# Fixing experts 0, 4 and 8 as the first three, and loading the third's gate and up into the out product's buffers

## The chip, the cores and the metric

The kernel is one program on one core of one Trainium2 chip. What counts is the device time of one execution in microseconds, the median over runs.

## What is computed

One step of a diffusion backbone with one layer: 128 context tokens and 256 latent tokens of width 1024 go through a normalisation, two token mixers side by side, one output projection, and a mixture of experts. Everything is float32. The change touches only the last part:

```python
def _moe(h, router_w, router_b, w_gate, w_up, w_down):      # h: 384 tokens x 1024
    scores = sigmoid(h @ router_w)                          # 16 experts
    sel = scores + router_b
    g = argmax over 4 groups of the sum of the group's two best sel
    expert = the two best of the four experts of group g    # 768 (token, expert) pairs
    w = scores of the two, divided by their sum
    hg = einsum('td,edf->tef', h, w_gate)                   # w_gate, w_up: 16 x 1024 x 512
    hu = einsum('td,edf->tef', h, w_up)
    act = silu(hg) * hu * gates
    return einsum('tef,efd->td', act, w_down)               # w_down: 16 x 512 x 1024
```

Gate and up of one expert are 2.10 MB each and its down matrix is 2.10 MB too, 6.29 MB in all; the sixteen are 100.7 MB.

## The kernel before

The kernel is written by hand, engine by engine; the order on each engine is that of the code, and engines meet at semaphores. SyncE (SP) issues nearly all loads, ScalarE (ACT) issues the writes of expert outputs, GpSimd (POOL) the indirect transfers. One large SBUF array, the arena, holds everything: nine slots of 16 KB per partition (`slot(0)` to `slot(8)`) and a region F behind them. What may be loaded when depends on who used the same bytes before.

**Up to the router.** The mixers' output is multiplied by w_out (L664), six products of a token tile and a half of the columns; each adds 1 to `wo_ready`. w_out lies in slots 7 and 8. VectorE then makes the normalised tokens h2 (slot 6, three tiles of 128 tokens), the router's product and the choice of two experts per token follow, and VectorE works out for each pair its row in a list of pairs sorted by expert (L1616 to L1646).

**The order of the experts.** The sorted list doesn't follow the experts' numbers. Each expert gets a key, its pair count times 32 plus a priority (`prio`). Two fixed experts, 0 and 1, have priorities so large that they come first. The number of larger keys is the expert's rank; from the rank a turn key is made, and the number of smaller turn keys is the expert's *place*, 0 to 15, in which it is worked on. Before, the turn key is 0.15 times the rank, plus 1 for ranks 2 and 4: places 0 to 15 hold the ranks 0, 1, 3, 5, 6, 7, 8, 2, 9, 10, 4, 11, 12, 13, 14, 15. `exp_i`, `n_i` and `off_i` hold, by place, the expert's number, its count and its first row.

**The sorted tokens.** GpSimd scatters h2's rows to their sorted rows in HBM (L1906, semaphore `tok_sent`). SP reads the 768 rows back as six tiles of 128 (`hsr`, L419, `hs_in0` to `hs_in5`), here into slot 7 and half of slot 8. TensorE transposes them (`sorted_columns`, L738, `hs_ready` counts two per tile), and ScalarE and VectorE copy half each out of PSUM (L1114, L1651). The expert in place 0 doesn't wait for this: its first 128 rows are gathered by a product with a one-hot matrix (L825, `first_ready`).

**The expert loop.** A place is worked on in passes of 64 rows, up to `PASSES` = 6, as many as the count needs; the others are `skipped`, which adds what they would have added to the semaphores. A pass on TensorE is `gate_up` (32 matmuls, L754), `down` of the pass before (16 matmuls, L767) and two transposes (L777). So the down of a place's last pass runs after the first gate_up of the next place. ScalarE does silu (L1110) and evacuates the output (L1125, L1129, two writes of 128 KB), VectorE multiplies (L1661), turns over (L1666) and stages the next 64 rows (`stage_x`, L1656).

**The weights.** There are `SETS` = 3 buffers, each with two slots for gate and up and one for down; place p uses buffer p mod 3. `reload` loads place p's gate and up once place p-3 has all its gate_ups counted (`gated`), and its down once place p-3's last down is counted (`downed`). The first two experts are known beforehand and load long before the router has run. The third is whatever the keys put in place 2: SP waits until it is known, loads its gate half after the sorted tiles are read, its up half and down when they are transposed (its buffer overlaps the tiles), and goes on with `reload` for places 3 to 15.

## Time and profile before

| | |
|---|---|
| median of 3 runs | 545.04 us (544.37 to 546.21) |
| span of the profiled execution, its own time | 544.1 us |
| TensorE (PE) matmuls busy | 480.4 us, 88% |
| VectorE (DVE) busy | 236.0 us, 43% |
| ScalarE (ACT) busy | 148.2 us, 27% |
| GpSimd (POOL) busy | 104.4 us, 19% |
| mean granted TensorE clock | 0.968 |
| HBM read and written | 152.77 MB and 11.34 MB |
| SP's loads of w_gate / w_up | 32 each of 1024 KB |
| SP's loads of w_down | 16 of 2048 KB |

The span runs from the first to the last instruction of one execution; the runs' times are measured from outside. Busy time is the sum of an engine's instructions and counts no waits. In rows of the timeline, the two numbers ahead of the engine are start and length in microseconds; in brackets stands how long the engine had been idle before and what released it. PEq, SPq and ACTq are the engines' instruction queues, at branches and at the issue of transfers. The granted clock is a share of TensorE's full 2.4 GHz: 1.00 is that, 0.50 is 1.2 GHz.

### The profile page before, as it was taken

The page shows a single profiled execution, that of the slowest core. Times are in us where ns is not written, and L with a number is a line of the kernel's source. Part 1 is how long each engine was busy: PE and PEld are TensorE (multiplying, and loading weights), DVE is VectorE, ACT ScalarE, POOL GpSimd, SP SyncE. Part 2 cuts the span into 40 slices and gives each one's busy share as a digit, 9 for nine tenths or more (in the row PEclk, how much of TensorE's full clock was granted, in tenths as well). Part 3 has the DMA queues.
Part 4 walks back from the last instruction along what each step waited for, and adds up shares of the span by engine and source line. Part 5 has one row for each costly group of instructions (what it writes and reads, how often), then busy time and mean ns, then how long its engine had stood idle before and what let it go on. Part 6 is the DMA issues. An engine that isn't in the chain of part 4 may idle for free. (4 is left out here: it accounts for less than half of the span.)

```text
span 544.1 us, 8978 instructions
## 1 busy us (share of the span) xinstructions
PE 480.4 (88%) x3278; PEld 233.3 (43%) x3279; DVE 236.0 (43%) x590; ACT 148.2 (27%) x289; POOL 104.4 (19%) x187
## 2 busy tenths in 40 slices
PE   2788979899969999995996999899998999999893
PEld 1135669655559644573344333333333333333331
DVE  2698994999963300867663101111011101111045
ACT  3645794532147610151102010110001100101142
POOL 3000250988870203500500000000000000000300
PEclk9988999999999999995998999999999999999998
DMA  8993046449497999220696999999999999999932
GB/s 278 339 400 112 1 154 217 166 166 363 143 391 269 369 366 417 82 86 1 239 385 243 410 423 418 418 418 416 421 421 419 419 417 419 417 420 421 403 120 116
DMA packets 42571, 164.64 MB, mean 303 GB/s; under 512 B 3314, under 2 KB 4106, under 8 KB 32676
## 3 DMA queue, kind: packets, MB, share of 16 engines
q1 hardware_dynamic: 35440, 144.22, 67.3%
q10 hardware_dynamic: 4580, 11.91, 5.8%
q0 software_dynamic: 2512, 7.99, 4.0%
q8 instruction: 24, 0.39, 0.3%
q14 instruction: 15, 0.12, 0.1%
HBM read 152.77 MB, written 11.34 MB: 302 GB/s over the span
## 5 line engine op out<-in xcount | busy, mean ns | idle before, releaser
L754 PE MATMUL psum<-arena 128*64 128x512 f32 x672 | 150.7, 601 | 16.7 <-DVE arena L1656 7.8
L754 PEld LDWEIGHTS psum<-arena 128*64 128x64 f32 x672 | 49.8, 138 | 103.7 <-issue 101.9
L767 PE MATMUL psum<-arena 128*64 128x512 f32 x336 | 75.9, 592 | 0.0
L1661 DVE TENSOR_TENSOR arena<-arena,psum 128x256 f32<-128x256 f32 x21 | 8.8, 421 | 143.4 <-ACT arena L1110 143.2
L1916 POOL DMA_INDIRECT arena<-sorted_outputs,src_u x6 | 5.7, 951 | 244.1 <-DMA sorted_outputs<-arena 242.6
L767 PEld LDWEIGHTS psum<-arena 128*64 128x64 f32 x336 | 25.7, 137 | 45.9 <-issue 45.9
L1110 ACT ACTIVATE arena<-psum 128x256 f32<-128x256 f32 x21 | 8.0, 383 | 130.0 <-PE psum L754 114.5
L664 PE MATMUL psum<-arena 128*128 128x512 f32 x96 | 42.2, 594 | 0.0
L1125 ACT ACTIVATE arena<-psum 128x512 f32<-128x512 f32 x19 | 11.3, 597 | 58.0 <-PE psum L767 58.0
L664 PEld LDWEIGHTS psum<-arena 128*128 128x128 f32 x96 | 17.9, 190 | 21.2 <-issue 20.9
L1656 DVE COPY arena<-arena 128x512 f32 x31 | 13.1, 423 | 30.4 <-issue 30.4
L487 PE MATMUL psum<-arena 128*2 128x512 f32 x64 | 18.4, 734 | 8.1 <-DMA arena<-in_w_mod 8.1
L528 PE MATMUL psum<-arena 128*128 128x388 f32 x64 | 23.8, 521 | 1.1 <-ACT arena L957 1.1
L940 ACT ACTIVATE arena<-arena 128x512 f32<-128x512 f32 x32 | 20.9, 715 | 7.7 <-DVE arena L1371 7.7
L536 PE MATMUL psum<-arena 128*128 128x388 f32 x64 | 21.1, 491 | 0.0
L617 PE MATMUL psum<-arena 128*128 128x512 f32 x48 | 20.9, 594 | 0.0
L1666 DVE COPY arena<-psum 128x256 f32<-128x256 f32 x21 | 8.9, 425 | 25.3 <-PEq L786 13.7
L1860 POOL TENSOR_TENSOR arena<-arena 128x64 f32<-128x64 f32 x32 | 14.8, 464 | 22.3 <-DVEq L1462 19.9
L472 PE MATMUL psum<-arena 128*2 128x128 f32 x512 | 15.4, 273 | 1.4 <-DMA arena<-in_w_mod 1.4
L528 PEld LDWEIGHTS psum<-arena 128*128 128x128 f32 x64 | 12.4, 203 | 9.0 <-issue 3.0
L1862 POOL TENSOR_TENSOR arena<-arena 128x64 f32<-128x64 f32 x32 | 15.2, 476 | 2.5
L536 PEld LDWEIGHTS psum<-arena 128*128 128x128 f32 x64 | 12.1, 190 | 8.4
(355 smaller groups left out, 657.3 us busy)
## 6 DMA issues: line engine op xcount, KB each, us to landing
arena<-in_w_gate SPq DMA_DIRECT2D x32, 1024.0 KB, 15.7
arena<-in_w_up SPq DMA_DIRECT2D x32, 1024.0 KB, 18.1
arena<-in_w_down SPq DMA_DIRECT2D x16, 2048.0 KB, 15.2
arena<-in_w_mod SPq DMA_DIRECT2D x12, 2048.0 KB, 13.0
arena<-in_w_in SPq DMA_DIRECT2D x3, 2048.0 KB, 19.2
sorted_outputs<-arena ACTq DMA_DIRECT2D x38, 128.0 KB, 6.3
arena<-in_w_out SPq DMA_DIRECT2D x2, 2048.0 KB, 16.7
arena<-modulation_rows ACTq DMA_DIRECT2D x4, 1024.0 KB, 10.7
```

What stands on the lines that cost most here:

```text
L472: last = mm(out[t], sil[:, k, :], w[:, k, t * P:t * P + P], start=(k == 0), stop=False)
L487: last = mm(bank[(4, 7)[c]][32 * t:32 * t + 2, :], sil[:, k, :], w[:, kk, t * D + c * 512:t * D + c * 512 + 512], start=(k == 0), stop=(k ...
L528: last = mm(bank[c][:, 0:TOK], w[:, k, c * P:(c + 1) * P], h1T[:, k, :], start=(k == 0), stop=(k == KD - 1))
L536: last = mm(out, w[:, k, c * P:(c + 1) * P], h1T[:, k, :], start=(k == 0), stop=(k == KD - 1))
L617: last = mm(bank[b][:, :], h1T[:, k, T0[t]:T0[t] + P], w[:, k, :], start=(k == 0), stop=(k == KD - 1))
L664: last = mm(bank[OUT_BANK[2 * t + h]][:, :], yT[:, k, T0[t]:T0[t] + P], wout[h][:, k, :], start=(k == 4), stop=(k == 3))
L754: last = mm(bank[0][HALF * t:HALF * t + HALF, :], xs[:, side, k, :], gu[:, :, k, t * 256:t * 256 + 256], start=(k == 0), stop=(k == KD - 1))
L767: last = mm(bank[4][HALF * h:HALF * h + HALF, :], hiddenT[:, s * P + t * HALF:s * P + t * HALF + HALF], dn[:, 2 * t + s, h * 512:h * 512 + ...
L940: last = A(out[:, :, 16 * g:16 * g + 16], made[i % 4], ACT.Copy, scale=side[:, c:c + 1])
L1656: cp(xs[:, side], hTs[:, :, bass.ds(row, HALF)]).then_inc(S("x_staged"), 1)
L1860: p(G.tensor_tensor(pt1, prev, Tre, ALU.mult))
L1862: w(G.tensor_tensor(nxt, nxt, pt1, ALU.add))
```

## The change

- The fixed experts are 0, 4 and 8 (`EARLY`), with priorities 65536, 32768 and 16384.
- The turn key becomes rank + 1.75 for ranks 0 to 9 and half the rank from 10 on.
- The third buffer's gate and up move from slots 6 and 7 to slots 7 and 8, its down from slot 8 to slot 6. SP loads the third expert's gate and up when the sixth out product is done.
- The six sorted tiles move: tiles 0, 1 and 2 lie where h2 was, tile 3 behind it over the router's small arrays, tile 4 in region F, and tile 5 shares tile 0's place. SP loads tiles 0, 1, 2, 4, then 3; ScalarE issues the load of tile 5 after tile 0 is transposed.
- Place 3's gate and up are issued when place 0 is counted off, ahead of the wait for the transposed tiles; the third's down comes after that wait, place 3's down when its buffer is free.
- On TensorE the branches of place 0 are rearranged: with two passes it counts the missing passes off between the second gate_up and its down, and again ahead of the sorted tiles' transposes, which now stand inside the branch.

```diff
--- before.py
+++ after.py
@@ -52,6 +52,7 @@
 OUT_BANK = (4, 5, 6, 7, 0, 1)
 SORT_BANK = ((1, 5), (6, 7), (3, 5), (6, 7), (3, 5), (6, 7))
 UNIT = 4096
+EARLY = (0, 4, 8)
 EPS = 1e-6
 PI = 3.141592653589793
 BIG = 1.0e30
@@ -162,7 +163,7 @@
         g2rows = view(slot(0) + 6144, 2, D)
         h2 = view(slot(6), NT, D)
         h2T = view(F + 3072, KD, NT * P)
-        hsr = view(slot(7), 6, D)
+        hsr = [view(at, D) for at in (slot(6), slot(6) + 1024, slot(6) + 2048, slot(6) + 3072, F + 12544, slot(6))]
         hTs = view(F + 3072, KD, READ)
         xs = view(F + 10752, 2, KD, HALF)
         first_rows = [view(F + 12544 + 512 * i, 512) for i in range(2)]
@@ -179,8 +180,8 @@
 
 
         def expert_weights(j):
-            b = (3, 0, 6)[j]
-            return view(slot(b), 2, KD, DE), view(slot(b + 2), 4, D)
+            gu, dn = ((3, 5), (0, 2), (7, 6))[j]
+            return view(slot(gu), 2, KD, DE), view(slot(dn), 4, D)
 
         cur = [F + 14928]
 
@@ -407,30 +408,36 @@
 
             sp.wait_ge(S("y_ready"), 4)
             sp.wait_ge(S("fin_done"), 1)
-            load_gate_up(0, 0)
-            load_down(0, 0)
+            load_gate_up(0, EARLY[0])
+            load_down(0, EARLY[0])
             sp.wait_ge(S("unit_used"), 15)
-            load_gate_up(1, 1)
+            load_gate_up(1, EARLY[1])
             sp.wait_ge(S("yt_done"), 4)
             sp.wait_ge(S("modd_in5"), 32)
-            load_down(1, 1)
+            load_down(1, EARLY[1])
+            sp.wait_ge(S("wo_ready"), 6)
+            load_gate_up(2, EARLY[2])
+
+            def load_sorted(t):
+                sp.dma_start(hsr[t], hsd[t * P:(t + 1) * P, :]).then_inc(S(f"hs_in{t}"), 16)
+
             sp.wait_ge(S("tok_sent"), 16 * 6)
-            for t in range(6):
-                sp.dma_start(hsr[:, t, :], hsd[t * P:(t + 1) * P, :]).then_inc(S(f"hs_in{t}"), 16)
-            sp.wait_ge(S("first_ready"), 1)
+            sp.wait_ge(S("pad_sent"), 48)
+            sp.wait_ge(S("first_ready"), 4)
+            for t in (0, 1, 2):
+                load_sorted(t)
+            load_sorted(4)
             sp.wait_ge(S("onehots_done"), 1)
-            sp.wait_ge(S("pad_sent"), 48)
             sp.wait_ge(S("int_done"), 1)
-            third = expert_at(2)
-            for k, sem in ((0, "gu_in2"), (KD // 2, "gu_rest2")):
-                sp.dma_start(expert_weights(2)[0][:, 0:1, k:k + KD // 2],
-                             wg[:, bass.ds(third, 1), k:k + KD // 2, :]).then_inc(S(sem), 16)
+            load_sorted(3)
+            fourth = expert_at(SETS)
+            sp.wait_ge(S("gated"), PASSES)
+            load_gate_up(0, fourth)
             sp.wait_ge(S("hs_ready"), 12)
-            for k, sem in ((0, "gu_in2"), (KD // 2, "gu_rest2")):
-                sp.dma_start(expert_weights(2)[0][:, 1:2, k:k + KD // 2],
-                             wu[:, bass.ds(third, 1), k:k + KD // 2, :]).then_inc(S(sem), 16)
-            load_down(2, third)
-            for e in range(SETS, NE):
+            load_down(2, EARLY[2])
+            sp.wait_ge(S("downed"), PASSES + 1)
+            load_down(0, fourth)
+            for e in range(SETS + 1, NE):
                 reload(e % SETS, e)
             sp.wait_ge(S("columns_copied"), 1)
             for ri, name in enumerate(("out_re", "out_im")):
@@ -736,7 +743,7 @@
                     for kk in range(4):
                         k = 4 * h + kk
                         last = tr(bank[SORT_BANK[t][h]][:, kk * P:(kk + 1) * P],
-                                  hsr[:, t, :].rearrange("p (q k) -> p k q", k=KD)[:, k, :], ident[:, :])
+                                  hsr[t].rearrange("p (q k) -> p k q", k=KD)[:, k, :], ident[:, :])
                     last.then_inc(S("hs_ready"), 1)
 
             pe.wait_ge(S("exp_done"), 1)
@@ -839,16 +846,43 @@
             pe.wait_ge(S("first_staged"), 2)
             pe.wait_ge(S("x_staged"), 2)
             first_n = pe.value_load(n_i[0:1, 0:1], min_val=0, max_val=NT * P)
+
+            def sorted_tiles():
+
+                for t in range(6):
+                    sorted_columns(t)
+                pe.wait_ge(S("hs_copied_a"), 6)
+                pe.wait_ge(S("hs_copied_v"), 6)
+
             with pe.If(first_n > HALF):
-                second_pass(0, 0, 0)
-            for t in range(6):
-                sorted_columns(t)
-            pe.wait_ge(S("hs_copied_a"), 6)
-            pe.wait_ge(S("hs_copied_v"), 6)
-            with pe.If(first_n > HALF):
-                later_passes(0, 0, 0, first_n)
+                gate_up(0, turn(1, 0), None, 1)
+                with pe.If(first_n > P):
+                    down(0, 1, turn(1, 0), turn(0, 0))
+                    transposes(turn(1, 0))
+                    sorted_tiles()
+                    gate_up(0, turn(2, 0), None)
+                    down(0, 1, turn(2, 0), turn(1, 0))
+                    transposes(turn(2, 0))
+                    with pe.If(first_n > P + HALF):
+                        with pe.Fori(3, PASSES) as q:
+                            gate_up(0, q + turn(0, 0), None)
+                            down(0, 1, q + turn(0, 0), q + turn(0, 0) + -1)
+                            transposes(q + turn(0, 0))
+                    with pe.Else():
+                        skipped(0, 3)
+                with pe.Else():
+                    pe.wait_ge(S("gated"), turn(2, 0))
+                    pe.sem_inc(S("gated"), PASSES - 2)
+                    down(0, 1, turn(1, 0), turn(0, 0))
+                    transposes(turn(1, 0))
+                    pe.wait_ge(S("crossed"), turn(2, 0))
+                    pe.wait_ge(S("downed"), turn(2, 0))
+                    pe.sem_inc(S("crossed"), PASSES - 2)
+                    pe.sem_inc(S("downed"), PASSES - 2)
+                    sorted_tiles()
             with pe.Else():
                 skipped(0, 1)
+                sorted_tiles()
             with pe.Fori(0, 5) as i:
                 for j in range(SETS):
                     e = i * SETS + j
@@ -1174,7 +1208,10 @@
             first_n = act.value_load(n_i[0:1, 0:1], min_val=0, max_val=NT * P)
             with act.If(first_n > HALF):
                 second_pass(0)
-            for t in range(6):
+            sorted_copy(0)
+            act.wait_ge(S("hs_ready"), 2)
+            act.dma_start(hsr[5], hsd[5 * P:6 * P, :]).then_inc(S("hs_in5"), 16)
+            for t in range(1, 6):
                 sorted_copy(t)
             with act.If(first_n > HALF):
                 later_passes(0, 0, first_n)
@@ -1558,10 +1595,10 @@
             row4 = desc[:, 12:16].unsqueeze(1).broadcast_to([P, NT, 4])
             d(V_.memset(chosen_row[:, NT * NE:], 0.0))
             d(V_.memset(before[:, 2 * NE:2 * NE + 1], 0.0))
-            d(V_.memset(prio[:, 0:1], 65536.0))
-            d(V_.memset(prio[:, 1:2], 32768.0))
             dve.wait_ge(S("tri_done"), 1)
-            d(cp(prio[:, 2:NE], desc[:, 2:NE]))
+            for i, e in enumerate(EARLY):
+                d(V_.memset(prio[:, e:e + 1], 65536.0 / 2 ** i))
+                d(cp(prio[:, e + 1:(*EARLY, NE)[i + 1]], desc[:, e + 1:(*EARLY, NE)[i + 1]]))
             dve.wait_ge(S("tri_done"), 4)
             for lot in range(2):
                 d(ts(counted_rows[lot], count_row, 1.0 + HALF * lot, None, ALU.add))
@@ -1616,11 +1653,11 @@
             v(stt(key, bank[3][:, NT * NE + 1:NT * NE + 1 + NE], 32.0, prio[:, :], ALU.mult, ALU.add))
             d(cp(counted, bank[3][:, NT * NE + 1:NT * NE + 1 + NE]))
             v(tt(larger, key.unsqueeze(1).broadcast_to(square), key.unsqueeze(2).broadcast_to(square), ALU.is_gt))
-            rank, turn_key = r1[:, 0, :], key
+            rank, turn_key, counted_rank = r1[:, 0, :], key, r2[:, 0, :]
             v(V_.tensor_reduce(rank, larger, AX.X, ALU.add))
-            v(ts(turn_key, rank, 0.15, None, ALU.mult))
-            for r in (2.0, 4.0):
-                v(stt(turn_key, rank, r, turn_key, ALU.is_equal, ALU.add))
+            v(ts(counted_rank, rank, 0.5, 1.75, ALU.mult, ALU.add))
+            v(stt(counted_rank, rank, 9.5, counted_rank, ALU.is_lt, ALU.mult))
+            v(stt(turn_key, rank, 0.5, counted_rank, ALU.mult, ALU.add))
             v(tt(larger, turn_key.unsqueeze(1).broadcast_to(square), turn_key.unsqueeze(2).broadcast_to(square), ALU.is_lt))
             v(tt(product, larger, counted.unsqueeze(1).broadcast_to(square), ALU.mult))
             v(V_.tensor_reduce(starts, product, AX.X, ALU.add))
```

## Rows read from the trace of the kernel before

**Rows 1.** Page, part 2: share of the DMA engines in 40 slices of 13.6 us

```profile
DMA  8993046449497999220696999999999999999932
```

**Rows 2.** Windows: stretch, length, busy time by engine, granted clock, DMA share, GB/s

```profile
241.00:257.00 16.00, 9.92 (x46) 7.46 (x46) 11.17 (x50) 4.15 (x7) 0.00 (x0) 0.55 0.00 1
...
299.00:356.00 57.00, 53.62 (x248) 18.72 (x246) 7.28 (x18) 5.71 (x14) 0.00 (x0) 1.00 1.02 418
...
410.00:507.10 97.10, 90.61 (x417) 31.95 (x417) 12.11 (x31) 9.26 (x23) 0.00 (x0) 1.00 1.02 419
```

**Rows 3.** Timeline of TensorE from the out product to the last place

```profile
233.45 3.60 PE L664 MATMUL psum<-arena 128*128 128x512 f32 x8
...
279.62 3.61 PE L767 MATMUL psum<-arena 128*64 128x512 f32 x16
...
293.58 8.78 PE L754 MATMUL psum<-arena 128*64 128x512 f32 x32 [3.62 <-DVE arena L1656]
...
306.88 7.09 PE L754 MATMUL psum<-arena 128*64 128x512 f32 x32 [0.72 <-PEq L786]
...
329.49 7.09 PE L754 MATMUL psum<-arena 128*64 128x512 f32 x32 [0.90 <-PEq L786]
...
341.43 7.09 PE L754 MATMUL psum<-arena 128*64 128x512 f32 x32 [1.05 <-DVE arena L1656]
...
353.03 7.09 PE L754 MATMUL psum<-arena 128*64 128x512 f32 x32 [0.72 <-PEq L786]
...
364.57 7.09 PE L754 MATMUL psum<-arena 128*64 128x512 f32 x32 [0.65 <-PEq L786]
...
376.49 7.09 PE L754 MATMUL psum<-arena 128*64 128x512 f32 x32 [1.03 <-DVE arena L1656]
...
409.91 7.09 PE L754 MATMUL psum<-arena 128*64 128x512 f32 x32 [0.89 <-PEq L786]
...
502.61 3.65 PE L754 MATMUL psum<-arena 128*64 128x512 f32 x16 [0.65 <-PEq L786]
507.10 3.65 PE L754 MATMUL psum<-arena 128*64 128x512 f32 x16 [0.83 <-DMA arena<-in_w_up]
```

**Rows 4.** DMA view of 291.3 to 507.1 us: totals, issues with median us to landing

```profile
DMA packets 17662, 89.99 MB, mean 417 GB/s; under 512 B 1632, under 2 KB 1632, under 8 KB 10623
...
sorted_outputs<-arena ACTq DMA_DIRECT2D x36, 128.0 KB, 6.4
arena<-modulation_rows ACTq DMA_DIRECT2D x1, 1024.0 KB, 9.0
```

**Rows 5.** Timeline of SP's queue

```profile
270.68 2.74 SPq L419 DMA_DIRECT2D arena<-sorted_tokens  x6
274.57 0.94 SPq L426 DMA_DIRECT2D arena<-in_w_gate  x2
289.99 0.81 SPq L430 DMA_DIRECT2D arena<-in_w_up  x2
...
292.12 0.34 SPq L389 DMA_DIRECT2D arena<-in_w_gate  x1
...
305.83 0.39 SPq L394 DMA_DIRECT2D arena<-in_w_down  x1
...
341.19 0.33 SPq L389 DMA_DIRECT2D arena<-in_w_gate  x1
```

**Rows 6.** Timeline of ScalarE and VectorE around the sorted tiles

```profile
284.04 1.32 ACTq L1129 DMA_DIRECT2D sorted_outputs<-arena  x2
...
290.00 0.69 DVE L1651 COPY arena<-psum 128x512 f32<-128x512 f32 x1 [0.20 <-PE psum L738]
...
293.01 0.43 DVE L1656 COPY arena<-arena 128x512 f32 x1 [2.32 <-issue]
```

**Rows 7.** DMA view of 270.6 to 270.9 us: the first sorted tile, us to landing

```profile
arena<-sorted_tokens SPq DMA_DIRECT2D x1, 512.0 KB, 3.2
```

**Rows 8.** Windows of TensorE alone: its busy time, granted clock, DMA share, GB/s

```profile
294.00:297.00 3.00, 3.00 (x10) 0.50 0.98 400
```

## The prediction, made before the changed kernel had run

> **What bounds the kernel now.** I read the busy tenths of the page first: the DMA engines stand still around 241 to 257 us and are full from about 291 us until shortly before the end [rows 1, 2]. That full stretch is the expert loop, so I then read TensorE and SP's queue in order of time.
>
> In the loop TensorE hardly waits. Place 1 starts at 293.58 and place 15, the last, at 502.61 [rows 3]. A place with one pass takes 11.54 us (353.03 to 364.57) or 11.92 (364.57 to 376.49), one with two 22.61 (306.88 to 329.49), one with three 33.42 (376.49 to 409.91) [rows 3]; so a further pass costs 10.8 us, and the gaps of 0.7 us between places are the branches. But the stream of weights is full for the same time. From 291.3 to 507.1 it moves 89.99 MB at 417 GB/s [rows 4], and at 507.10 TensorE waits 0.83 us for the second half of the last expert's gate and up [rows 3]. Two chains thus end together: TensorE's (start of place 1 plus the places) and the stream's (bytes plus the time it is dry). Whichever ends later at place 15 sets the end; behind it 37 us follow that the change leaves alone.
>
> Passes by place are read from those starts: 2, 1, 2, 1, 1, 1, 1, 3, 1, 1, 2, 1, 1, 1, 1, 1, so 21. The trace names no expert. Working the reference's router through on its own inputs gives 108, 37, 143, 90, 9, 41, 48, 32, 16, 18, 12, 4, 63, 52, 18, 77 pairs for experts 0 to 15; put in the order of the old turn keys and cut into lots of 64 that is the same row of passes, so I trust it for the new keys.
>
> **The new order.** The fixed three get ranks 0, 1, 2. Turn keys are rank + 1.75 up to rank 9 and half the rank from 10, which sorts the ranks as 0 1 2 3 10 11 4 12 13 5 14 15 6 7 8 9. With the counts above the passes become 2, 1, 1, 3, 1, 1, 2, 1, 1, 2, 1, 1, 1, 1, 1, 1. Still 21, still 2 in place 0, so TensorE's work from place 1 to 15 stays 209.0 us. What moves is where the long places stand: three passes already in place 3.
>
> **The edits that cost nothing.** The rank arithmetic is one tensor_scalar and two scalar_tensor_tensor of 16 columns on either side. The two further memsets and copies into prio are a few tenths of a microsecond that VectorE does while it waits for the router's product; without that cover they would cost that much. The new SP waits ahead of the tile loads (pad_sent, first_ready 4) are met before 270.68, where the tokens' scatter lets SP go now [rows 5]. Only the reads of tile 3 and the weights are queued behind onehots_done and int_done, both over by then.
>
> **The third expert's early gate and up.** They wait for the sixth out product, over at 237.05 [rows 3], and their 4.19 MB take 10.0 us at 418 GB/s in a stretch where the DMA share is 0.00 [rows 2]. Today the gate half is issued at 274.57 and the up half at 289.99 [rows 5]. So 4.19 MB leave the busy part, and place 3's gate and up can be issued once place 0 is counted off, at about 280.0 (its second gate_up ends as the down at 279.62 starts [rows 3]) and not at 292.12 [rows 5].
>
> **Tile 5, the new wait.** It has no buffer of its own any more: ScalarE issues its load after tile 0 is transposed. TensorE's count-off now stands between the second gate_up and its down, and again before the sorted tiles. The nearest row is the 0.72 us branch gap ahead of 306.88 [rows 3]; bounds 0 and 1.6 for both, taken 0.8. ScalarE today ends the issue of the evacuation's writes at 285.36 [rows 6]; with 0.8 and one copy of 0.6 it issues tile 5 at 286.8. At that time 4.19 MB of place 3 are in SP's queue since 280.0. From 281.5 the engines have 4.19 + 0.26 (writes) + 0.52 MB (tile 5) = 4.98 MB, 11.9 us, so all is through at 293.4. Landing times: 3.2 us for 512 KB with nothing ahead, 6.4 for 128 KB and 9.0 for 1024 KB beside a full SP queue [rows 4, 7]. Between the last two I take 7.0: landing at 293.8. Then 1.0 us of transposes and the copy, whose start goes from 290.00 [rows 6] to 294.8. The 2.3 us of VectorE's branches and stage_x come after it as now [rows 6]. Place 1 therefore starts 4.8 us later, at 298.4. Bounds: 286.0 + 3.2 gives +0.2; 287.6 + 9.0 gives +7.6. On ScalarE the copy of tile 1 is queued behind the new wait and the issue, some 0.6 us, and TensorE's tile 3 waits for that copy; tiles 1 to 4 are still done by about 291, ahead of the landing. On SP the weights of place 3 stand behind the wait for the count-off, and the third's down behind hs_ready; neither is needed before place 3 and 4.
>
> The Trainium skill (DMA: Bandwidth & Descriptors, Queues, rings and completion order) says that each DMA engine takes turns between the queues that have work, a packet at a time. By that ScalarE's load would get half the bandwidth, and the sum would be that of the fair-share rival below, 2.5 us less.
>
> **TensorE's clock.** Now it idles 3.62 us ahead of place 1, the granted clock is 0.50 from 294 to 297, and the first gate_up takes 8.78 us where others take 7.09 [rows 3, 8]. After the change it idles too, in two pieces around tile 5's transposes. I keep the 1.7 us; bounds: 1.7 less if it does not fall, and about as much again if each idle piece is followed by a slow stretch.
>
> **The stream, step by step.** The down of place 3 is issued when place 1's down is over: now 305.83, 12.25 after the start of place 1 [rows 3, 5]; then 310.7. Before it only 2.1 MB (the third's down) follow place 3's gate and up, so the stream is dry from about 301 to 311. Place 2 starts at 298.4 + 13.3 = 311.7, place 3 (one pass before it now) at 323.2, place 4 (three passes) at 356.7. Meanwhile the stream can carry the down of 3 and experts 4 and 5, 14.7 MB and 1 MB of writes, and is done near 350; expert 6 needs the buffer that place 3 holds. So it is dry for another 8 us. Today the three passes stand in place 7, after four single ones in which the stream had fallen behind, and no dry time shows [rows 1].
>
> A place's first gate load is issued 0.24 us before the next place starts (341.19 against 341.43 [rows 3, 5]); for expert 6 that is 356.5, and data flow 1.5 us later, 358.0. From there to the last gate and up it carries experts 6 to 14 and that, 9 x 6.29 + 4.19 = 60.8 MB, 13 passes of writes, 3.4 MB, and the two broadcast loads at the end, 1.57 MB: 65.8 MB, 157.4 us at 418 GB/s. It ends at 515.4 where it ends at 507.1 now.
>
> TensorE would reach place 15 at 298.4 + 209.0 = 507.4. Its first half of weights lands 5.0 us before the last, at 510.4 (wait 3.0), the second at 515.4 (wait 1.3). The sum: 4.8 (tile 5) + 4.3 (new waits) - 0.8 (the old one) = **+8.3 us**. The profiled execution spans 544.1, so 552.4; the median of the runs, 545.04, is 0.9 above it, so **553.3 us**.
>
> **Rivals.**
> 1. *Fair share.* Tile 5 gets half of 418 GB/s: 2.5 us, and 1.95 of fixed time (3.2 less 1.25 for its bytes) make 4.5, landing at 291.3. All behind it is 2.5 earlier: +5.8, 550.8 us. Against it: 1024 KB by this would take 7.0, the row has 9.0 [rows 4]. The skill's rule named above speaks for it.
> 2. *TensorE alone bounds.* The stream keeps up, as it would if it were not dry in place 3. Then only the late start counts: 4.8 - 0.8 = +4.0, 549.0 us. It needs 4.3 us less of stream, 2.7% more than 418 GB/s; the long stretches show 418 and 419 [rows 2].
> 3. *Not slower: no bubble at place 1.* Tile 5 is in place when TensorE gets to it (landed by 289.0), place 1 starts at 293.6, and its first gate_up runs at 2.4 GHz, so place 4 starts at 350.2. The stream ends at 508.9: +1.8, 546.8 us, the edge of no difference. It decides if place 2 starts by 305.0 (306.88 now). Only a landing near the 3.2 us floor would do that, beside a queue with 4 MB in it.
> 4. *The head start wins.* From 281.5 all that is left is 88.9 MB, 212.7 us: a stream never dry would end at 494.2. TensorE could then save its 0.8 us and the slow clock's 1.7, 542.5 us, if tile 5 were in time as well. Over 12.9 us of dry time undo it, and I count 18.
>
> **Chances and range.** Forecast 0.52, with a range of its own of 551 to 556; fair share 0.20; TensorE alone 0.12; no bubble 0.10; head start 0.04; worse than all, 0.02. From 548 to 557 us holds the first three and the upper bound of tile 5 but for its last microsecond. What a measurement tells from no change is 0.3%, 1.6 us: faster 0.05, same 0.09, slower 0.86.
>
> **What would show it.** SP issues gate and up twice at about 237 and at 280; TensorE idles ahead of the last eight sorted transposes, and place 1 starts near 298 (right: tile 5; at 294: rival 3). In the places, the three passes come third, with TensorE starts near 323 and 357. The DMA share falls in two dips, near 301 to 311 and 350 to 358, and TensorE waits for in_w_up or in_w_gate some 4 us at place 15 (none: rival 2). A start of place 1 near 296 with the same dips is rival 1. I am wrong altogether if the passes by place are others than listed.

## The result, and the profile after

The change makes the kernel slower, and by more than twice what was forecast: 564.3 us median (562.93 to 568.6, 4 runs) against 545.62 (544.37 to 546.48), a ratio of 1.036 with a 95% interval of 1.031 to 1.041. The forecast was 553.3, its range 548 to 557. The profiled execution is the slowest of the four, with a span of 566.9 us, 22.8 over that of [rows 1 to 8]; the others span 561.2 to 563.7. The account below is made for that execution and is therefore some 4 us larger than the median's 18.7.

The busy share of the DMA engines first, from part 2 of the page, in 40 slices of 14.2 us:

```profile
DMA  8991045649497994463684599299999999999922
```

The early load fills the slices from 227 us on that were low in [rows 1], and in return there are holes: an 8, a 4 and a 5 from 284 to 326 us, and a 2 at 354 to 368. TensorE in order of time (start, length, and in brackets the idle time before with its releaser):

```profile
265.94 7.09 PE L761 MATMUL psum<-arena 128*64 128x512 f32 x32
...
282.54 3.65 PE L774 MATMUL psum<-arena 128*64 128x512 f32 x16 [0.30 <-PEq L875]
...
287.22 4.70 PE L745 MATMUL psum<-arena 128*128 128x128 f32 x40 [0.66 <-PEq L881]
297.99 1.97 PE L745 MATMUL psum<-arena 128*128 128x128 f32 x8 [6.07 <-DMA arena<-sorted_tokens]
303.58 9.97 PE L761 MATMUL psum<-arena 128*64 128x512 f32 x32 [3.61 <-DVE arena L1693]
...
318.02 7.09 PE L761 MATMUL psum<-arena 128*64 128x512 f32 x32 [0.66 <-PEq L793]
...
333.60 8.62 PE L761 MATMUL psum<-arena 128*64 128x512 f32 x32 [4.70 <-PEq L794]
...
368.94 7.09 PE L761 MATMUL psum<-arena 128*64 128x512 f32 x32 [1.27 <-DVE arena L1693]
...
522.35 6.38 PE L761 MATMUL psum<-arena 128*64 128x512 f32 x16 [3.70 <-DMA arena<-in_w_up]
529.96 3.65 PE L761 MATMUL psum<-arena 128*64 128x512 f32 x16 [1.23 <-DMA arena<-in_w_up]
```

Four things are to be seen that [rows 3] do not have. The eight transposes of tile 5 wait 6.07 us for the tile. Place 1 then starts at 303.58, and its first gate_up takes 9.97 us. Ahead of place 3 (333.60) TensorE idles 4.70 us, put down to its own queue, and the gate_up behind takes 8.62 us and not 7.09. And place 15 waits 3.70 and 1.23 us for its weights, with a slow first half (6.38 us for 16 matmuls, 3.65 elsewhere) between. SP's queue over the same stretch:

```profile
238.04 0.33 SPq L390 DMA_DIRECT2D arena<-in_w_gate  x1
...
273.59 2.25 SPq L422 DMA_DIRECT2D arena<-sorted_tokens  x5
282.52 0.35 SPq L390 DMA_DIRECT2D arena<-in_w_gate  x1
...
300.00 17.41 SPq L395 DMA_DIRECT2D arena<-in_w_down  x2
```

The third expert's gate and up are issued at 238.04 and the fourth's at 282.52, as the change wants. Tile 5, from the DMA view of 280 to 300 us (the first line is the DMA share in 40 steps of 0.5 us, the second the median us from issue to landing):

```profile
DMA  9963000989899999999999999999899910000000
...
arena<-sorted_tokens ACTq DMA_DIRECT2D x1, 512.0 KB, 9.6
```

It takes 9.6 us. The engines are full until about 296. Which of the two queues has them is told by the queue rows of the DMA view (q1 is SP's queue, q10 ScalarE's; packets, MB, share of the 16 engines), first for 291 to 294 us, then for 295 to 298:

```profile
q1 hardware_dynamic: 142, 1.03, 81.7%
q10 hardware_dynamic: 139, 0.25, 21.8%
...
q10 hardware_dynamic: 120, 0.43, 35.8%
q1 hardware_dynamic: 15, 0.01, 0.9%
```

While both have work they move the same number of packets, 142 and 139, but SP's are of 8 KB, those of ScalarE's two writes of 2 KB and those of the tile of 4 KB. So ScalarE's queue has a fifth of the time and not a half. Its two writes stand ahead of the tile, whose first packets run at 294.0, and 104 of its 128 packets run after 295.0, when SP's 4.19 MB are through. Last the windows (stretch, length, TensorE's busy time, granted clock, DMA share, GB/s):

```profile
300.00:311.00 11.00, 7.42 (x22) 0.57 0.55 194
311.00:320.00 9.00, 8.34 (x40) 1.00 0.22 50
...
352.00:358.00 6.00, 6.00 (x30) 1.00 0.76 307
358.00:372.00 14.00, 12.73 (x62) 1.00 0.30 90
372.00:500.00 128.00, 120.37 (x556) 1.00 1.01 415
```

50 GB/s at 311 to 320 and 90 at 358 to 372 are the two dry stretches of the stream; from 372 on it is full again at 415.

**The account.** Before stands for [rows 3], after for the rows above, in us:

| piece | before | after | difference, us |
|---|---|---|---|
| start of place 0's first gate_up | 263.50 | 265.94 | +2.4 |
| from there to the start of place 1 | 30.08 | 37.64 | +7.6 |
| place 1 (slow clock in its first gate_up) | 13.30 | 14.44 | +1.1 |
| place 2, one pass | 11.54 | 15.58 | +4.0 |
| place 3, three passes | 33.83 | 35.34 | +1.5 |
| places 4 to 14, 13 passes, without waits | 150.36 | 150.36 | 0.0 |
| place 15's waits and slow half | 0.83 | 7.0 | +6.2 |
| from its second half to the end | 37.0 | 36.9 | -0.1 |

The "before" of place 2 is the one-pass place of [rows 3], and the 150.36 are the 161.18 of places 4 to 14 (341.43 to 502.61) less one pass of 10.82. The 33.83 of place 3 is what is then left of the 209.03 from place 1 to place 15 in [rows 3]; the place with three passes there took 33.42, and e5 below, which has them in place 3 without the stall, 33.79 (330.06 to 363.85). The differences add up to 22.8.

The slow half of place 15 costs nothing of its own: TensorE waits another 1.23 us behind it for the second half's weights, so the 6.2 us are the stream's.

The first line of the account can't be put down to the change. TensorE's granted clock fell at about 241 us:

```profile
241.00:242.00 1.00, 1.00 (x7) 0.58 1.02 434
...
304.00:308.00 4.00, 4.00 (x12) 0.50 0.83 334
```

(0.50 is its 1.2 GHz level, 1.00 the 2.4 GHz one; the second line is place 1's first gate_up), so the router's products ran slower. In the kernel before it fell too, but some 1.5 us later, and was back some 2 us sooner. In the experiments below place 0's first gate_up starts between 260.3 and 265.9 us, without any link to which kernel it is (e1, without the early load, had the slow products too; e3, with it, started at 260.27).

### The profile page after: what moved, and what is told of

Same layout as the page of the kernel before. It is cut to its first block and busy times, and to the rows that moved or that the text cites. A ratio compares the mean times of both kernels' runs of the same rounds, so it can differ in the third digit from the quotient of the medians.

```text
span 566.9 us, 8972 instructions
## 1 busy us (share of the span) xinstructions
PE 489.7 (86%) x3278; PEld 237.7 (42%) x3279; DVE 236.8 (42%) x593; ACT 148.5 (26%) x289; POOL 103.9 (18%) x187
## 5 line engine op out<-in xcount | busy, mean ns | idle before, releaser
L761 PE MATMUL psum<-arena 128*64 128x512 f32 x672 | 156.2, 618 | 24.1 <-DVE arena L1693 8.5
L774 PE MATMUL psum<-arena 128*64 128x512 f32 x336 | 75.9, 593 | 0.3 <-PEq L875 0.3
L671 PEld LDWEIGHTS psum<-arena 128*128 128x128 f32 x96 | 17.9, 190 | 21.2 <-issue 20.9
## 6 DMA issues: line engine op xcount, KB each, us to landing
arena<-in_w_gate SPq DMA_DIRECT2D x32, 1024.0 KB, 13.3
```

Source lines behind the costliest of these rows:

```text
L671: last = mm(bank[OUT_BANK[2 * t + h]][:, :], yT[:, k, T0[t]:T0[t] + P], wout[h][:, k, :], start=(k == 4), stop=(k == 3))
L761: last = mm(bank[0][HALF * t:HALF * t + HALF, :], xs[:, side, k, :], gu[:, :, k, t * 256:t * 256 + 256], start=(k == 0), stop=(k == KD - 1))
L774: last = mm(bank[4][HALF * h:HALF * h + HALF, :], hiddenT[:, s * P + t * HALF:s * P + t * HALF + HALF], dn[:, 2 * t + s, h * 512:h * 512 + ...
```

## The experiments

Twelve kernels ran. Beside each median stands that of before, measured together with it. Differences between two experiments are of what each has over its own before.

| run | passes by place | median (before) | ratio, 95% interval | place 1 after place 0 starts, us | idle ahead of place 3 | waits at place 15 |
|---|---|---|---|---|---|---|
| before | 2 1 2 1 1 1 1 3 1 1 2 1 1 1 1 1 | | | 30.08 | 0.90 | 0.83 |
| the change | 2 1 1 3 1 1 2 1 1 2 1 1 1 1 1 1 | 564.3 (545.62) | 1.036 (1.031 to 1.041) | 37.64 | 4.70 | 3.70 + 1.23 |
| e1 | as the change | 557.87 (546.7) | 1.022 (1.015 to 1.030) | 30.09 | 4.73 | 3.73 + 2.22 |
| e2 | 2 1 1 2 1 1 1 1 3 1 1 2 1 1 1 1 | 559.09 (546.7) | 1.020 (1.013 to 1.028) | 38.14 | 4.71 | none |
| e3 | as the change | 558.06 (546.7) | 1.023 (1.015 to 1.031) | 31.01 | 4.67 | 4.89 + 0.25 |
| e4 | as the change | 557.76 (546.7) | 1.020 (1.013 to 1.028) | 30.49 | 4.73 | 3.71 + 1.03 |
| e8 | 2 1 1 1 1 1 3 1 2 1 2 1 1 1 1 1 | 550.67 (545.64) | 1.012 (1.006 to 1.017) | 29.96 | 4.66 | none |
| e5 | 2 1 2 3 1 1 2 1 1 1 1 1 1 1 1 1 | 562.74 (545.64) | 1.031 (1.025 to 1.037) | 30.49 | 0.89 | 4.93 + 2.20, and at places 12 to 14 |
| e6 | 2 1 2 1 1 1 1 3 1 2 1 1 1 1 1 1 | 552.1 (545.64) | 1.011 (1.008 to 1.015) | 30.63 | 0.96 | 2.30 |
| e7 | as e6 | 559.32 (545.64) | 1.027 (1.023 to 1.030) | 38.52 | 0.89 | 2.38 |
| e9 | 2 1 2 1 1 1 1 1 3 1 2 1 1 1 1 1 | 545.28 (545.35) | 1.001 (0.998 to 1.004) | 30.47 | 0.89 | none |
| e10 | as before | 550.94 (545.35) | 1.012 (1.008 to 1.016) | 33.24 | 0.90 | none |
| e11 | as e9 | 552.25 (545.35) | 1.014 (1.011 to 1.017) | 34.34 | 0.90 | none |
| e12 | as e9 | 549.58 (546.67) | 1.006 (1.003 to 1.009) | 31.74 | 0.89 | none |

**e1: the keys alone.** The kernel before with the priorities and turn keys of the change (the edit of `prio` and `EARLY`, which is that of the change, is left out here).

```diff
-            v(ts(turn_key, rank, 0.15, None, ALU.mult))
-            for r in (2.0, 4.0):
-                v(stt(turn_key, rank, r, turn_key, ALU.is_equal, ALU.add))
+            v(ts(counted_rank, rank, 0.5, 1.75, ALU.mult, ALU.add))
+            v(stt(counted_rank, rank, 9.5, counted_rank, ALU.is_lt, ALU.mult))
+            v(stt(turn_key, rank, 0.5, counted_rank, ALU.mult, ALU.add))
```

> The kernel before with nothing but the new priorities and turn keys (experts 0 and 4 loaded beforehand, the third still loaded once it is known). Theory (the three-pass expert in place 3 lets the weight stream run dry): place 1 still starts near 293.6 us, the DMA share dips while place 3 works on its three passes (near 343 to 352), place 15 waits some 3 to 4 us for weights, and the time is 3 to 5 us over before, near 549. Rival (the late start of place 1 explains all, the order costs nothing): no wait at place 15 and 545.

Measured: 557.87 us, 2.2% over before: more than half of the loss, and two to three times what I had put on the order. TensorE's timeline of e1:

```profile
291.49 8.42 PE L755 MATMUL psum<-arena 128*64 128x512 f32 x32 [3.62 <-DVE arena L1657]
...
304.37 7.09 PE L755 MATMUL psum<-arena 128*64 128x512 f32 x32 [0.67 <-PEq L787]
...
319.99 9.52 PE L755 MATMUL psum<-arena 128*64 128x512 f32 x32 [4.73 <-PEq L788]
...
509.66 5.12 PE L755 MATMUL psum<-arena 128*64 128x512 f32 x16 [3.73 <-DMA arena<-in_w_up]
517.00 3.65 PE L755 MATMUL psum<-arena 128*64 128x512 f32 x16 [2.22 <-DMA arena<-in_w_up]
```

The waits at place 15 are there, 3.73 and 2.22 us, where I had expected 3 to 4 in all. What I had not expected is the third line: place 3 starts 15.6 us after place 2, not 11.6, and its gate_up is slow. So this stall came with the keys, not with the buffers.

**e2: the long experts late.** The change with other turn keys:

```diff
-            v(ts(counted_rank, rank, 0.5, 1.75, ALU.mult, ALU.add))
-            v(stt(counted_rank, rank, 9.5, counted_rank, ALU.is_lt, ALU.mult))
-            v(stt(turn_key, rank, 0.5, counted_rank, ALU.mult, ALU.add))
+            v(ts(turn_key, rank, 0.15, None, ALU.mult))
+            for r in (3.0, 5.0):
+                v(stt(turn_key, rank, r, turn_key, ALU.is_equal, ALU.add))
```

> The changed kernel with turn keys in the old manner (0.15 times the rank, plus 1 for ranks 3 and 5), so that the three passes stand in place 8 and place 3 has two... places 0 to 15: 2,1,1,2,1,1,1,1,3,1,1,2,1,1,1,1 passes. Theory (order starves the stream): the wait at place 15 (5 us and 2.7 of slow clock in the changed kernel) is gone, about 558 us, while place 1 still starts near 303. Rival (order costs nothing): unchanged, 564.

Measured: 559.09 us, and TensorE's timeline has no wait for weights at place 15:

```profile
302.28 9.42 PE L761 MATMUL psum<-arena 128*64 128x512 f32 x32 [3.62 <-DVE arena L1693]
...
519.01 7.09 PE L761 MATMUL psum<-arena 128*64 128x512 f32 x32 [0.69 <-PEq L793]
```

That is the theory's picture and its time within 1.1 us. The late start of place 1 and the stall ahead of place 3 remain.

**e3: nothing beside tile 5's load.**

```diff
-            sp.wait_ge(S("gated"), PASSES)
-            load_gate_up(0, fourth)
             sp.wait_ge(S("hs_ready"), 12)
+            sp.wait_ge(S("gated"), PASSES)
+            load_gate_up(0, fourth)
             load_down(2, EARLY[2])
```

> The changed kernel, but place 3's gate and up are issued after all sorted tiles are transposed, so nothing stands beside tile 5's load. Theory (4 MB beside it make tile 5 land after 9.4 us): it lands in about 4, place 1 starts 5 to 6 us sooner, and as the stream was dry later on anyway the time falls by about that, to 559. Rival (the load is slow by itself, or the bubble has another cause): tile 5 still takes over 8 us and the time stays or grows.

Measured: 558.06 us. Tile 5's row in e3's DMA view, and TensorE around it:

```profile
arena<-sorted_tokens ACTq DMA_DIRECT2D x1, 512.0 KB, 3.8
```

```profile
281.54 4.71 PE L745 MATMUL psum<-arena 128*128 128x128 f32 x40 [0.66 <-PEq L881]
286.51 1.16 PE L745 MATMUL psum<-arena 128*128 128x128 f32 x8 [0.26 <-DMA arena<-sorted_tokens]
291.28 9.38 PE L761 MATMUL psum<-arena 128*64 128x512 f32 x32 [3.61 <-DVE arena L1693]
```

3.8 us to landing where the change had 9.6: it was the weights beside it, not ScalarE's queue. TensorE waits 0.26 us, and place 1 starts 31.01 us after place 0. The time is 11.4 us over before where the change has 18.7: 7.3 less (6.2 in the medians as they stand, 5 to 6 expected), although place 3's weights are issued much later: they were not needed that early.

**e4: a place of its own for tile 5.** Tile 5 in slot 2, loaded by SP with the others; expert 4's down, which lay there, is loaded after the tiles are transposed.

```diff
-        hsr = [view(at, D) for at in (..., F + 12544, slot(6))]
+        hsr = [view(at, D) for at in (..., F + 12544, slot(2))]
...
-            load_down(1, EARLY[1])
             sp.wait_ge(S("wo_ready"), 6)
...
             load_sorted(4)
+            load_sorted(5)
...
             sp.wait_ge(S("hs_ready"), 12)
+            load_down(1, EARLY[1])
             load_down(2, EARLY[2])
```

> The changed kernel with tile 5 in slot 2 and loaded by SP with the others; expert 4's down, which had slot 2, is loaded after the tiles are transposed. Theory (tile 5's wait is the late start): no idle time inside the sorted transposes, place 1 starts near 296 (before 293.6, plus 1 for the count-off and some for an upstream delay), the time is near 556. Rival (contention of the place 3 loads would delay something else in its stead): place 1 still starts after 300.

Measured: 557.76 us. Place 1 starts 30.49 us after place 0, so of the 7.6 us only 0.4 are left, which fits TensorE's count-off: its profile has 0.30 us idle ahead of the second pass's down and 0.66 ahead of the transposes, where before had 0.77 among the transposes. The time is 11.1 us over before, 7.6 less than the change has; it is 1.8 us above what I expected, within the interval of the ratio.

**e8: place 2 with one pass, in the kernel before.** One number is added, and place 2 gets a one-pass expert.

```diff
-            for r in (2.0, 4.0):
+            for r in (2.0, 3.0, 4.0):
```

> The kernel before with the turn key's plus 1 for ranks 2, 3 and 4, so that place 2 has one pass where it had two: passes 2,1,1,1,1,1,3,1,2,1,2,1,1,1,1,1, same buffers, same loads. Theory (TensorE's branch over the unused passes of place 2 leads into instructions that are not there yet, and it waits for them): TensorE idles 4.7 us ahead of place 3 with an instruction transfer inside the gap, the gate_up behind it takes 8.5 to 10 us, and the time is 4 to 6 us over before, 551. Rival (the stall belongs to the early or late weight loads of the changed kernel): place 3 starts 11.6 us after place 2, and the time is within 1 us of before, 546.

Measured: 550.67 us. TensorE's timeline, and the instruction row of the DMA view of 318 to 323.3 us (transfers, MB, share of 16 engines):

```profile
307.66 7.09 PE L754 MATMUL psum<-arena 128*64 128x512 f32 x32 [0.67 <-PEq L786]
...
323.21 8.67 PE L754 MATMUL psum<-arena 128*64 128x512 f32 x32 [4.66 <-PEq L787]
```

```profile
q8 instruction: 1, 0.02, 1.2%
```

The same stall, 4.66 us, in a kernel that has none of the new buffers, and the 8.67 us gate_up behind it; no wait at place 15. The kernel is 5.0 us over before. In the change the DMA view of the gap, 329 to 333.2 us, has one such transfer too:

```profile
q8 instruction: 1, 0.02, 1.5%
```

In the kernel before the transfer falls in 319 to 320 us,

```profile
q8 instruction: 1, 0.02, 6.2%
```

while place 2's second pass is at work [rows 3], and TensorE doesn't wait. A transfer in a gap is no sign by itself: before has one at 329 to 330 us too, in the 0.90 us ahead of place 3. What goes with the stall is the timing. In the change, e1, e2, e3, e4 and e8 a transfer starts 1.4 to 1.5 us after TensorE's last transposes of place 2, and TensorE goes on 3.2 to 3.4 us after the transfer's start. And the stall stays in the loop's first turn: from 355 to 540 us the change has no transfer of this queue at all, and the gaps behind its one-pass places are 0.65 to 0.67 us there, or 1.08 to 1.30 where the loop goes back. The view names no engine for the queue q8; that it is TensorE's is my reading.

The Trainium skill (Runtime: NRT & Kernel Launch, Instruction fetch mechanics) says that an engine's instructions come in blocks of 16 KiB by DMA, read ahead in sequence, and that a branch taken to a block that isn't there has to wait for it. The rows agree in each point that they can show: 0.02 MB a transfer, and the stall where the branch over the unused passes is taken before the code behind it has come. I had read that branch as 0.7 us from places where the code was already there. That place 2's missing second pass alone brings the stall is shown; that the wait is for these instructions rests on the timing.

**e5: place 2 with two passes.** e4 with expert 15 fixed in the stead of 8 (and the copy behind the last fixed expert left out, as there is nothing behind 15).

```diff
-EARLY = (0, 4, 8)
+EARLY = (0, 4, 15)
```

> e4 (tile 5 in slot 2) with expert 15 fixed in place 2 in the stead of 8, so that place 2 has two passes: 2,1,2,3,1,1,2,1,1,1,1,1,1,1,1,1. Theory (instruction stall of place 2's branch): the 4.7 us gap ahead of place 3 and the slow clock behind it are gone, but the three passes stand in place 3 and the last double one in place 6, so the stream still runs dry and place 15 waits longer than in e4; in all 552 to 556. Rival (the stall stays): 558.

Measured: 562.74 us. The stall is gone (0.89 us), but the time is 7 us over the top of what I expected. TensorE's timeline of e5:

```profile
293.31 9.69 PE L762 MATMUL psum<-arena 128*64 128x512 f32 x32 [3.62 <-DVE arena L1692]
...
330.06 7.09 PE L762 MATMUL psum<-arena 128*64 128x512 f32 x32 [0.89 <-PEq L794]
...
468.16 3.65 PE L762 MATMUL psum<-arena 128*64 128x512 f32 x16 [0.65 <-DMA arena<-in_w_up]
472.99 3.65 PE L762 MATMUL psum<-arena 128*64 128x512 f32 x16 [1.18 <-DMA arena<-in_w_up]
...
483.52 5.03 PE L762 MATMUL psum<-arena 128*64 128x512 f32 x16 [3.08 <-DMA arena<-in_w_up]
...
499.31 5.35 PE L762 MATMUL psum<-arena 128*64 128x512 f32 x16 [2.73 <-DMA arena<-in_w_up]
...
517.37 5.17 PE L762 MATMUL psum<-arena 128*64 128x512 f32 x16 [4.93 <-DMA arena<-in_w_up]
524.74 3.65 PE L762 MATMUL psum<-arena 128*64 128x512 f32 x16 [2.20 <-DMA arena<-in_w_up]
```

Nine one-pass places in a row, 7 to 15, come last, and the stream delivers one expert in 15.7 us (6.29 MB and 0.26 of writes at 418 GB/s) where TensorE uses one in 11.7. From place 12 on each place waits. The dry stretch while place 3 worked is not made up for. From the start of place 1 to the second half of place 15 e5 takes 231.4 us (293.31 to 524.74), before 213.5 [rows 3]; 0.9 of the 17.9 is place 1's slow clock. So the order costs 17 us here, the whole of the loss, and far more than I had sized.

**e6: all three causes taken away.** e5 with other turn keys.

```diff
-            v(ts(counted_rank, rank, 0.5, 1.75, ALU.mult, ALU.add))
-            v(stt(counted_rank, rank, 9.5, counted_rank, ALU.is_lt, ALU.mult))
-            v(stt(turn_key, rank, 0.5, counted_rank, ALU.mult, ALU.add))
+            v(ts(turn_key, rank, 0.18, None, ALU.mult))
+            for r in (3.0, 4.0):
+                v(stt(turn_key, rank, r, turn_key, ALU.is_equal, ALU.add))
```

> e5 with turn keys 0.18 times the rank plus 1 for ranks 3 and 4: passes 2,1,2,1,1,1,1,3,1,2,1,1,1,1,1,1, nearly those of before. Theory (tile 5's wait, the branch stall and the dry stream are the whole loss): no stall, no long wait at place 15, 545 to 547, no gain over before since TensorE's chain sets the end. Rival (something else in the change costs time too): 549 or more.

Measured: 552.1 us, 1.1% over before: the rival's time, and the theory missed. No stall, no long wait ahead of place 15, but 2.30 us in the middle of it, with 1.7 us of slow clock behind. TensorE then idles 1.97 us ahead of the last transposes, where e9 has 0.68, and runs slow again behind; what it waits for there isn't settled. From the second half of place 15 to the end it is 41.5 us, 37.0 before. Its second double stands in place 9, that of before in place 10. That left open whether the order alone was enough; e9 was made for it.

**e7: tile 5 alone.** e6 with tile 5 as the change has it: in slot 6, issued by ScalarE behind its first copies, and expert 4's down early.

```diff
-        hsr = [view(at, D) for at in (..., F + 12544, slot(2))]
+        hsr = [view(at, D) for at in (..., F + 12544, slot(6))]
...
-            load_sorted(5)
...
-            for t in range(6):
+            sorted_copy(0)
+            act.wait_ge(S("hs_ready"), 2)
+            act.dma_start(hsr[5], hsd[5 * P:6 * P, :]).then_inc(S("hs_in5"), 16)
+            for t in range(1, 6):
                 sorted_copy(t)
```

> The changed kernel with the fixed experts and turn keys of e6, but tile 5 as the change has it (tile 0's place, loaded by ScalarE). Theory: place 1 starts 7.6 us later relative to place 0's first gate_up, with 1 us of slow clock more; the place 2 stall is gone; 553 to 555. Rival (the stream's head start pays the late start back): 547 to 549.

Measured: 559.32 us, 7.2 over e6. Tile 5's load took 8.7 us, TensorE waited 5.15 for it. Place 1 starts 7.9 us later after place 0 than in e6, near the 7.6 of the account, though 1.7 of it are a slow clock in place 0's second gate_up (8.78 us), which e6 doesn't have. My absolute number was off by 4, as e6's was by 5.

**e9: the long experts nearly in the places of before.**

```diff
-            v(ts(turn_key, rank, 0.18, None, ALU.mult))
+            v(ts(turn_key, rank, 0.15, None, ALU.mult))
```

This puts three passes in place 8 and two in place 10.

> e6 with turn keys 0.15 times the rank plus 1 for ranks 3 and 4: passes 2,1,2,1,1,1,1,1,3,1,2,1,1,1,1,1, so that the second double stands in place 10 as in the kernel before (e6 had it in place 9 and place 15 waited 2.3 us with 1.7 of slow clock behind). Theory (the places of the long experts decide whether the stream is in time): no wait at place 15, 545 to 547. Rival (the 6 us that e6 lost have another cause): 550 or more.

Measured: 545.28 against 545.35 us over 12 and 17 runs. TensorE's timeline has no stall ahead of place 3 and no wait in place 15:

```profile
291.03 9.66 PE L762 MATMUL psum<-arena 128*64 128x512 f32 x32 [3.62 <-DVE arena L1692]
...
327.75 7.09 PE L762 MATMUL psum<-arena 128*64 128x512 f32 x32 [0.89 <-PEq L794]
...
500.97 7.09 PE L762 MATMUL psum<-arena 128*64 128x512 f32 x32 [0.69 <-PEq L794]
```

With tile 5 out of the way, two passes in place 2, and the other long experts within one place of where before had them, what is left of the change (the early gate and up, the new buffers, the count-off) neither costs nor gains anything beyond 0.4%. The passes of e6 and e9 differ in nothing but the places 7 to 10, so the 6 us that e6 loses are the order's.

**e10, e11, e12: keeping TensorE busy ahead of place 1.** In all kernels above TensorE idles 3.6 us there, and the gate_up that follows takes 8.4 to 10.0 us, not 7.1. I put matmuls whose result is never read into that time: 8 in the kernel before (e10), 8 in e9 (e11), 4 in e9 (e12).

```diff
                 for t in range(6):
                     sorted_columns(t)
+                pe.wait_ge(S("gu_in1"), 32)
+                for _ in range(8):
+                    mm(bank[0][:, :], ident[:, :], expert_weights(1)[0][:, 0, 0, :], start=True, stop=True)
```

> The kernel before with 8 further matmuls of 512 columns, whose result is never read, behind the sorted transposes, so that TensorE is busy for most of the 3.6 us in which it waited for place 1. Theory: the granted clock stays 1.00 and place 1's gate_up takes 7.1 us where it took 8.8, but the weight stream, full from 291 to 507 us, then sets the end alone: within 1 us of before. Rival (TensorE's chain sets the end): 1.7 us or more faster, 543.5.

> e9 with the same 8 matmuls. Theory: here the stream has its head start of 2 MB, so the 1.7 to 2.8 us of slow clock come off the time: 2 us under e9 and 1 to 2 under before, 544. Rival (the stream is just in time in e9 as well): same as e9.

Measured: 550.94 and 552.25 us, both over 1% slower than before. TensorE's timeline of e10:

```profile
287.95 7.03 PE L848 MATMUL psum<-arena 128*128 128x512 f32 x16
294.91 7.09 PE L754 MATMUL psum<-arena 128*64 128x512 f32 x32
...
345.29 8.84 PE L754 MATMUL psum<-arena 128*64 128x512 f32 x32 [5.26 <-DVE arena L1659]
```

Place 1's gate_up does take 7.09 us. But the 8 matmuls are 16 in the trace, with 16 weight loads, and take 7.0 us, so place 1 starts 3 us later; and there is a new gap of 5.26 us, ahead of place 4, with an instruction transfer in it and 1.75 us of slow clock behind. The row puts the gap down to VectorE's copy, but VectorE had itself waited for TensorE's queue:

```profile
344.46 0.42 DVE L1669 COPY arena<-psum 128x256 f32<-128x256 f32 x1 [4.86 <-PEq L786]
```

Both experiments are thus spoilt as tests of which chain sets the end.

> e9 with 4 further matmuls in the stead of e11's 8 (each is two instructions and took 0.88 us, so 3.5 us and 8 instructions, not 7.0 and 16). e11 started place 1 some 3.4 us late and had a 4.5 us gap ahead of place 4 with an instruction transfer in it, at the loop's way back. Theory (the clock dip is worth 1.7 to 2.6 us; the gap comes from where the instruction blocks end): place 1's gate_up takes 7.1 us and starts no later than in e9; if no new gap appears, 543, if the shift by 8 instructions still puts the way back in front of a missing block, 547 to 548. Rival (the clock dip costs nothing in the end): same as e9, 545.3, with no gap.

Measured: 549.58 us. Place 1's gate_up takes 7.09 us and starts 1.3 us later than in e9, and the gap ahead of place 4 is there again (4.46 us, then a gate_up of 10.09). TensorE's loop goes back to its start between places 3 and 4. Eight matmuls with eight weight loads, put in ahead of the loop, were enough for that way back to wait, which fits with blocks that end elsewhere; I didn't test it by moving the blocks in any other way. What the slow clock ahead of place 1 costs in the end stays open.

## Why the prediction was wrong

**Direction and two of the mechanisms: right.** Slower was forecast at 0.86. The passes by place are those worked out from the router's counts. The stream runs dry twice, where the prediction said, and place 15 then waits: 3.70 and 1.23 us against 3.0 and 1.3. e2 and e9 show that the order of the passes is its cause: with the long experts late the waits are gone. But the profiled execution is 22.8 us over before where the sum had 8.3. The 14.5 us between them are the branch's stall with its slow clock (5.6), tile 5 (2.8), the stream's end at place 15 (2.7), place 1's clock (1.1), and the late start of place 0 (2.4), which can't be put down to the change.

**The first step that failed: "Place 2 starts at 298.4 + 13.3 = 311.7, place 3 (one pass before it now) at 323.2".** I took a one-pass place at 11.5 us wherever it stands. In place 2 it took 15.58: TensorE stands still for 4.0 us more at the branch over the unused passes, and the slow clock behind it adds 1.5. e1 shows it with the keys alone, e8 in the kernel before with nothing else, and e5, e6, e7 and e9 show it gone with two passes in place 2. That the code behind the branch had not come yet fits the timing of the instruction transfers. It was no rival and no bound. In the kernel before place 2 had two passes, so [rows 3] hold no such row; that such a branch can have to wait for its code is stated by the Trainium skill (Runtime: NRT & Kernel Launch, Instruction fetch mechanics) and was not in my sum.

**The second: tile 5's landing, taken as 7.0 us.** It was 9.6 (8.7 in e7, 10.2 in e2), beyond the 9.0 that I had as the upper bound. ScalarE issued it 0.9 us sooner after place 0 than I had it, and TensorE, idle for 6.07 us by then, did its eight transposes at a granted clock of 0.50, in 1.97 us and not 1.16 (e3). In all the term was 4.8 us and measured 7.6 in the profiled run, 7.2 between e6 and e7, 7.3 and 7.6 as what e3 and e4 save. The prediction had a better number in hand: it worked out that all 4.98 MB would be through at 293.4, which with everything 2.4 us later is 295.8, and adding the 1.95 us of fixed time gives 297.8; TensorE's transposes started at 297.99. By the same working e7 would have had the tile at 295.6 and e2 at 296.1; it landed at 294.7 and 296.7. Instead I interpolated between rows of other sizes. It came so because SP's queue had nothing behind the 4.19 MB: most of the tile ran once that was through. e3 settles that it is the weights beside it: 3.8 us with nothing there. (By the prediction's own sum the upper bound of tile 5 makes 556.1, all of it inside the range.)

Where the prediction cites the Trainium skill (DMA: Bandwidth & Descriptors, Queues, rings and completion order) for queues that take turns a packet at a time, the trace agrees, with 142 and 139 packets in the same 3 us. What failed is the step from there to "half the bandwidth": with packets of 8 KB against 2 KB ScalarE's queue had 0.25 of 1.28 MB, a fifth, and the tile stood behind two writes in that queue. The fair-share rival's 4.5 us is excluded by the 9.6 us.

**The third: the stream's 157.4 us.** From the first data of place 6's gate and up to the second half of place 15 it took 161.2 us (368.8 to 530.0), since it moved 66.62 MB at 413 GB/s and not 65.8 at 418. That it began 1.4 us sooner after place 4's start than I had it gives a part back. The idle times of 3.70 and 1.23 us look nearer to the forecast's 3.0 and 1.3 than they are: between them the first half ran slow while its second half's weights were still to come, so that place 15 lost 6.2 us where I had 3.5.

**The fourth, small: TensorE's clock.** Kept as before, it cost 1.1 us more in place 1 (9.97 us where before had 8.78), within the spread that the experiments show for the same idle time, 8.42 to 10.03. The bound of "as much again" covers it.

**The order's price in general.** The sum had 4.3 - 0.8 = 3.5 us for the order and nothing for the branch. e1 has no late start and still loses 11 us: 5.9 more than before in place 15's waits, and about 5 the stall with its clock (5.0 in e8; 6.5 in e1's own profile, whose place 0 started 2.1 us sooner than before's).

**The rivals.** TensorE alone as the bound, no bubble at place 1, and the head start are all excluded: the trace has the waits at place 15, the idle time in the transposes, and both dry stretches.

**Where the median's 18.7 us are.** The keys 11.2 (e1: stall and slow clock some 5, waits at place 15 some 6), tile 5 7.2 to 7.6 (e3, e4, e7). That is 18.4 to 18.8, and e9 says that nothing else is left beyond 0.4%.

## What to carry to other kernels

When each buffer is filled again only after its use, the order of long and short jobs decides whether the weight stream keeps up: a long job early, before the stream has fallen behind, leaves it dry, and a row of short jobs at the end leaves no time to catch up. A small load beside megabytes in another queue doesn't have half of the engines: look at the packets of both and at what stands ahead of it in its own queue. Where the other queue then runs empty, the time at which all of it is through plus the fixed time was a good price here, within 0.9 us in three kernels. And a branch's cost read from a later turn of a loop need not hold in the first one: a change that alters which branches are taken there added 4 us and the slow clock behind it, so look for gaps put down to the engine's own queue and at when the instruction transfers start.

## What the runs showed of the hardware

- TensorE's wait on its own queue at the branch behind place 2, put down here to instructions not yet read, was 4.66 to 4.73 us in six kernels with one pass in place 2 (the change, e1, e2, e3, e4, e8) against 0.65 to 0.96 elsewhere, and 4.46 to 5.26 us at the loop's way back in e10, e11 and e12, where the others have 1.0 to 1.3. In all nine gaps a transfer of 0.02 MB starts 0.8 to 1.5 us into the gap, and TensorE goes on 3.2 to 3.7 us after it. No such transfer came in the loop's later turns (355 to 540 us in the change).
- 512 KB issued by ScalarE landed after 3.8 us alone and after 8.7 to 10.2 us beside 4.19 MB that SP had issued 4 to 6 us before. While both queues had work they moved the same number of packets, 142 and 139 in 3 us, and by their sizes of 8 and 2 KB 1.03 and 0.25 MB (142 and 138 in e7).
- After 3.6 us of idle time ahead of place 1 the granted clock was 0.50 for a stretch, and 32 matmuls took 8.42 to 10.03 us, not 7.09; the spread between runs of nearly the same timing (8.78 in before, 10.03 in e8) had no cause that I could find.
